# Two programs in one launch: grouped attention's scores as three products of upper parts and rests, with the order of norms, finishes and loads changed

## The reference

```python
def first_block(...):          # two layers; layer 0 mLSTM, layer 1 sliding-window attention
    for i in range(DEPTH):
        u  = _modulate(_rms_norm(h,  norm_mix[i]), mod_l[0], mod_l[1])
        uc = _modulate(_rms_norm(hc, norm_mix[i]), mod_c[0], mod_c[1])
        ...                    # y, yc = _mlstm_mixer(...) or _swa_mixer(...)
        h = h + mod_l[2] * y
        h = h + mod_l[5] * _sq_relu_mlp(_modulate(_rms_norm(h, norm_ffn[i]), mod_l[3], mod_l[4]), w1, w2)
        ...                    # the context alike, in layer 0 only
    return _rms_norm(h, final_norm)

def attend(q, k, v):           # 8 query heads in 2 groups, width 64; queries and keys normed, latents' turned by rope
    s = jnp.einsum('btgrd,blgd->bgrtl', q, k, preferred_element_type=jnp.float32) * (ATTN_HEAD_DIM ** -0.5)
    p = jax.nn.softmax(s, axis=-1)
    return jnp.einsum('bgrtl,blgd->btgrd', p.astype(v.dtype), v)

def trunk_layer(...):          # second program, two layers
    h = x * (1.0 + scale) + shift
    y_attn = blocked_attention(ql, k_all, v_all) * jax.nn.silu(a_g)   # "grouped attention"
    ...                        # y_gla: gated linear attention; y_sgu: spatial gating unit
    out = merge(y_attn, y_gla, y_sgu, m_a, m_g, m_s)
    return layer_norm(DEEPNORM_ALPHA * x + gate * out, p['post_g'], p['post_b'])
```

## Time and profile before

| | |
|---|---|
| median of three runs | 3317.05 us (3314.15 to 3317.81) |
| profiled execution | 3313.33 us; its span 3311.5 us |
| TensorE busy | 3080.0 us, 93% |
| weight loads busy | 2560.9 us, 77% |
| VectorE busy | 1906.8 us, 58% |
| ScalarE busy | 1193.3 us, 36% |
| GpSimd busy | 210.8 us, 6% |
| HBM | 97 GB/s over the span |

### The profile page before, as it was taken

The page is one execution under the profiler, slowest core; times in us unless marked ns, Lnnn a source line. Parts: engine busy times, 40 slices in busy tenths (PEclk is TensorE's granted clock), DMA queues, the critical chain, the costliest instruction groups (busy, mean ns, idle before and its releaser), DMA issues.

```text
span 3311.5 us, 43104 instructions
## 1 busy us (share of the span) xinstructions
PE 3080.0 (93%) x17878; PEld 2560.9 (77%) x17878; DVE 1906.8 (58%) x2778; ACT 1193.3 (36%) x1810; POOL 210.8 (6%) x138
## 2 busy tenths in 40 slices
PE   7998899999997888999989999998899999998899
PEld 6787778888886666778877888886688777876677
DVE  7775646656524475688754444367444565455656
ACT  4225342212223354422235344335322454443432
POOL 0002100000010000000000222000000022200000
PEclk9999899999998899999989999999999999999999
DMA  5454124333321100355523222310212333230223
GB/s 215 154 188 145 39 66 132 126 123 125 111 64 58 39 1 24 130 189 187 184 87 74 78 77 77 114 43 1 86 58 76 109 102 104 98 117 20 70 93 127
DMA packets 100090, 323.91 MB, mean 98 GB/s; under 512 B 14310, under 2 KB 20326, under 8 KB 98744
## 3 DMA queue, kind: packets, MB, share of 16 engines
q1 hardware_dynamic: 89812, 291.29, 27.1%
q10 hardware_dynamic: 10084, 29.87, 2.5%
HBM read 301.46 MB, written 19.66 MB: 97 GB/s over the span
## 4 chain that ended last, share of the span: by engine, by line
PE 80%; DVE 9%; ACT 5%; issue 3%; DMA 1%; POOL 1%; SPq 0%; ACTq 0%; DVEq 0%; POOLq 0%
PE PS L393 79%; PE PS L396 1%; DVE STs L1390 1%; ACT Pq L1348 1%; ACT whi L198 1%; DVE wlo L212 1%; ACT Ps L1348 1%; DVE STq L1390 1%; DMA Ht<-in_hT 1%; POOL rows L2675 0%; POOL rows L2677 0%; DVE JUNK L546 0%; DVE mH L1160 0%; DVE STs L1397 0%; DVE q0t L2302 0%
## 5 line engine op out<-in xcount | busy, mean ns | idle before, releaser
L393 PE MATMUL PS<-U,whi 128*128 128x512 f32 (+1 forms) x5120 | 1091.3, 361 | 46.4 <-DVE U L673 20.4
L393 PEld LDWEIGHTS PS<-U,whi 128*128 128x128 f32 x5120 | 858.4, 191 | 218.9 <-issue 44.6
L212 DVE TENSOR_TENSOR wlo<-stage,whi 128x1024 fp32r<-128x1024 f32 x339 | 432.3, 1277 | 871.8 <-ACT whi L198 870.9
L198 ACT ACTIVATE whi<-stage 128x1024 fp32r<-128x1024 f32 x339 | 357.3, 1056 | 1031.9 <-PE PS L393 960.1
L393 PE MATMUL PS<-U,wlo 128*128 128x512 f32 (+1 forms) x2560 | 571.4, 356 | 0.0
L393 PEld LDWEIGHTS PS<-U,wlo 128*128 128x128 f32 x2560 | 431.7, 189 | 76.4
L393 PE MATMUL PS<-Y,whi 128*128 128x512 f32 (+1 forms) x2112 | 471.6, 359 | 12.1 <-DVE Y L2324 4.5
L393 PEld LDWEIGHTS PS<-Y,whi 128*128 128x128 f32 x2112 | 358.0, 189 | 79.8 <-issue 5.5
L393 PE MATMUL PS<-whi,U 128*128 128x512 f32 (+2 forms) x1152 | 324.2, 369 | 7.5 <-ACT g1qk L1846 4.6
L393 PE MATMUL PS<-Y,wlo 128*128 128x512 f32 (+1 forms) x1056 | 265.6, 358 | 0.0
L393 PEld LDWEIGHTS PS<-whi,U 128*128 128x128 f32 x1152 | 206.5, 190 | 49.2 <-ACT g1qk L1846 5.0
(11 more groups left out here) (433 smaller groups left out, 3137.9 us busy)
## 6 DMA issues: line engine op xcount, KB each, us to landing
stage<-in_w SPq DMA_DIRECT2D x128, 512.0 KB, 4.0
stage<-in_ada SPq DMA_DIRECT2D x80, 512.0 KB, 3.8
stage<-in_adb SPq DMA_DIRECT2D x48, 512.0 KB, 3.8
stage<-in_p_mg SPq DMA_DIRECT2D x16, 512.0 KB, 3.7
stage<-in_p_ma SPq DMA_DIRECT2D x16, 512.0 KB, 3.7
stage<-in_p_ms SPq DMA_DIRECT2D x16, 512.0 KB, 3.7
stage<-in_wo SPq DMA_DIRECT2D x16, 512.0 KB, 3.6
GS<-FS ACTq DMA_DIRECT2D x20, 384.0 KB
```

The lines of the kernel that those rows point to most:

```text
L198: act.activation(self.parts[r % n][0], self.stage[i % len(self.stage)], ACT.Copy).then_inc(*self.S.up("w_hi", i))
L212: dve.tensor_tensor(lo, self.stage[i % len(self.stage)], hi.bitcast(F32), ALU.subtract).then_inc(*self.S.up("w_lo", i))
L393: return pe.matmul(o, l, r, start=start, stop=stop_, skip_group_check=True)
```

## The change

Grouped attention's scores become three products of fp32r parts (`passes`): upper query·upper key, upper·rest, rest·upper. The queries' and keys' parts are made in the projections' stage; the queries' lie in `Y4`, where the results come later. SWA keeps float32, with one pass. The order in the attention loop changes: ScalarE's `finish` goes ahead of its copy of the turned weights; VectorE's is parted into `take` (the gating, grouped attention only) and `finish`, one round later. SWA's masks become one product of the identity with a band of up to 384 columns a head. In norms 0, 1 and 2 the first block is made in two parts, latents first. The final norm and the entry are interleaved, and the modulation there moves from VectorE to ScalarE. In mLSTM two of VectorE's rests of weights come between the scans. SP loads two tiles fewer before SWA's tables. `B.n` is set differently in SWA and grouped attention. In the grouped projections the turn comes one step later and a third gate tile goes into the loop.

```diff
-        def pe_pair(pe, tiles, x, xt):
+        def pe_pair(pe, tiles, x, xt, first=None):
 
 
             ss = [B.take(pe, i, *until) for i, _, until in tiles]
-            for k in range(8):
+            if first:
+                for a, b in cols(True):
+                    pe.wait_ge(*at(*(xt[0] if a else first)))
+                    for (i, _, _), s in zip(tiles, ss):
+                        wh, wl = W.views(i, 8)
+                        if a == 0:
+                            pe.wait_ge(*at("w_lo", i))
+                        for q, (xr, wv) in enumerate(((0, wh), (1, wh), (0, wl))):
+                            mm(pe, s[:, a:b], wv[:, 0, :], x(xr, 0, a, b), q == 0, False)
+            for k in range(1 if first else 0, 8):
...
-            for k in range(9):
+            if full:
+                for lo, hi, v in groups(True):
+                    part = (r, 0) if v else (r, "a")
+                    act.wait_ge(*at("n_mul", *part))
+                    act.activation(T1[0][:, lo:hi], T1[0][:, lo:hi], ACT.Identity, bias=mod(L, ish, 0, v),
+                                   scale=MU[:, 8 * v:8 * v + 1]).then_inc(*up("n_mod", *part))
+                    act.wait_ge(*at("n_mod", *part))
+                    act.activation(U[:, 0, 0, lo:hi], T1[0][:, lo:hi], ACT.Copy).then_inc(*up("n_hi", *part))
+            for k in range(1 if full else 0, 9):
...
+                if k == 0 and full:
+                    for lo, hi, v in groups(True):
+                        dve.tensor_tensor(T1[0][:, lo:hi], HT[:, 0, lo:hi], B.of(("root", r))[:, lo:hi], ALU.mult).then_inc(
+                            *up("n_mul", r, 0 if v else "a"))
+                elif k < 8:
                     if k >= 4:
                         dve.wait_ge(*at("n_lo", r, k - 4))
                     dve.tensor_tensor(T1[k % 4][:, 0:N], HT[:, k, 0:N], B.of(("root", r))[:, 0:N], ALU.mult).then_inc(
                         *up("n_mul", r, k))
-                if k >= 2:
+                if k == 1 and full:
+                    first(0, LAT, (r, "a"))
+                if k == 2 and full:
+                    first(LAT, TOK, (r, 0))
+                elif k >= 2:
...
+            dve_lo(dve, T("mqk", 0))
             gate(dve.tensor_tensor(mAR[r40, :], mIR[r40, :], mF[r40, :], ALU.subtract))
             gate(dve.memset(mMR[r40, :], 0.0))
             both(mMR, mAR, ALU.max)
+            dve_lo(dve, T("mqk", 1))
             gate(dve.tensor_tensor(mMM[r40, :], mF[r40, :], mMR[r40, :], ALU.add))
 
             for rows, c0, c1, before in ((slice(0, 8), 1, 4, 127), (slice(0, 8), 0, 1, 767), (slice(0, 8), 5, 6, 639),
@@ -1080,7 +1114,7 @@
                 top = chunks_of(mMR[rows, :])[:, :, end:end + 1].to_broadcast([8, 6, 128])
                 ins = dve.tensor_tensor(chunks_of(mWR[rows, :]), chunks_of(mAR[rows, :]), top, ALU.subtract)
             ins.then_inc(*up("m_rows"))
-            for j in range(8):
+            for j in range(2, 8):
...
-                            for h, s in enumerate(ss):
-                                last = mm(pe, s[:, c:c + m], a.query(gi, j, h, q0), a.keys(gi, h, k0, m), c % 512 == 0, True)
+                            for i, (query, keys_) in enumerate(a.passes):
+                                for h, s in enumerate(ss):
+                                    last = mm(pe, s[:, c:c + m], query(gi, j, h, q0), keys_(gi, h, k0, m),
+                                              c % 512 == 0 and i == 0, True)
                             c, k0, kn = c + m, k0 + m, kn - m
-                    for c, mask in masks:
+                    for n_, l, r in masks:
                         for s in ss:
-                            last = mm(pe, s[:, c:c + 128], mask[0], mask[1], False, True)
+                            last = mm(pe, s[:, 0:n_], l, r, False, True)
...
-                if n == 3:
-                    rest(act)
+                if n in (3, 4):
+                    rest(act, n - 3)
...
+                if 0 <= n - 2 < N and (n - 2) % 4 == 3:
+                    finish(act, (n - 2) // 4)
...
-        def dve_attention(dve, a, behind, rest, finish):
+
+        def dve_attention(dve, a, behind, rest, take, finish):
+
+
 
             N = len(a.jobs)
-            for n in range(N + 2):
-                if n == 3:
-                    rest(dve)
+            for n in range(N + 3):
+                if n in (3, 4):
+                    rest(dve, n - 3)
...
+                if 0 <= n - 3 < N and (n - 3) % 4 == 3:
+                    finish(dve, (n - 3) // 4)
...
+                if 0 <= n - 2 < N and (n - 2) % 4 == 3 and take:
+                    take(dve, (n - 2) // 4)
...
-                    if j >= 6:
-                        B.n = j
+                    if j == 6:
+                        B.n = 0
                     pe_proj(pe, T("sqk", j), xU, False, ("s_qk", j))
                 if n:
                     r = S_ORDER[n - 1]
-                    if j == 7:
-                        B.n = 0
                     pe_rope(pe, ("s", r), sRM[:, :], swa_turned(r), ("s_qk", r))
...
+            act.wait_ge(*at("ctx_in"))
+            act.wait_ge(*at("u_gain", 0, 1))
             for k in range(9):
                 if k < 8:
                     a = UN[k % 4]
-                    dve.wait_ge(*at("h_final", k))
+                    act.wait_ge(*at("h_final", k))
+                    if k >= 4:
+                        act.wait_ge(*at("u_lo", 0, k - 4))
                     for lo, hi, v in groups(True):
-                        ins = dve.tensor_scalar(a[:, lo:hi], HT[:, k, lo:hi], MU[:, 8 * v + k:8 * v + k + 1],
-                                                mod(2, 0, k, v), ALU.mult, ALU.add)
+                        ins = act.activation(a[:, lo:hi], HT[:, k, lo:hi], ACT.Identity, bias=mod(2, 0, k, v),
+                                             scale=MU[:, 8 * v + k:8 * v + k + 1])
                     ins.then_inc(*up("u_mod", 0, k))
                 if k:
-                    dve.wait_ge(*at("u_hi", 0, k - 1))
-                    dve.tensor_tensor(U[:, 1, k - 1, :], UN[(k - 1) % 4], U[:, 0, k - 1, :].bitcast(F32),
-                                      ALU.subtract).then_inc(*up("u_lo", 0, k - 1))
+                    act.wait_ge(*at("u_mod", 0, k - 1))
+                    act.activation(U[:, 0, k - 1, :], UN[(k - 1) % 4], ACT.Copy).then_inc(*up("u_hi", 0, k - 1))
...
+            dve_root(dve, 4, 4)
+            dve.wait_ge(*at("root", 4))
+            for k in range(10):
+                if k < 8:
+                    dve.scalar_tensor_tensor(HT[:, k, 0:LAT], HT[:, k, 0:LAT], col("final_norm", k),
+                                             B.of(("root", 4))[:, 0:LAT], ALU.mult, ALU.mult).then_inc(*up("h_final", k))
...
+                self.KS = [place(n + "kh", [128, TOK], F32R, offY2)[:, :], place(n + "kl", [128, TOK], F32R, offZ + 34848)[:, :]]
+
+                def query(r):
+                    return lambda gi, j, h, q0: Y4[64 * h:64 * h + 64, r, j, q0:q0 + 128]
+
+                def keys(r):
+                    return lambda gi, h, k0, m: self.KS[r][64 * h:64 * h + 64, k0:k0 + m]
+
+                self.attn = Attention(n, o1, 1, tiles, [(query(0), keys(0)), (query(0), keys(1)), (query(1), keys(0))],
                                       lambda gi, h, b: self.V[:, b, 64 * h:64 * h + 64])
...
-            for n in range(7):
+            for n in range(8):
+                if n == 7:
+                    B.n = 0
                 if n < 5:
                     pe_proj(pe, T(f"p_aqk{L}", n), xU, G.wide_at(n), ("q_z", L, n))
                 else:
@@ -2219,18 +2282,17 @@
                     for a, b in cols(m == TOK):
                         last = mm(pe, s[:, a:b], BONES, x[:, a:b], True, True)
                     last.then_inc(*up("q_ms", L, n - 1))
-                if n >= 2:
-                    if n == 2:
+                if n >= 3:
+                    if n == 3:
                         pe.wait_ge(*at("rot_in", L + 1))
-                    pe_rope(pe, (L, n - 2), G.RM, G.z(n - 2)[0][:, 0:512], ("q_nz", L, n - 2))
-            B.n = 2
-            for j in range(2, 4):
-                pe_proj(pe, T(f"p_ag{L}", j), xU, G.full, ("q_g", L, j))
+                    pe_rope(pe, (L, n - 3), G.RM, G.z(n - 3)[0][:, 0:512], ("q_nz", L, n - 3))
+            B.n = 3
+            pe_proj(pe, T(f"p_ag{L}", 3), xU, G.full, ("q_g", L, 3))
 
             def behind(pe):
                 pe_values(pe, ("q_v", L), [T(f"p_av{L}", 0)], 128, ("q_v", L))
 
-            pe_attention(pe, G.attn, {0: [("r_done", L, 4)]}, behind, ("q_v", L), lambda m: ("q_y", L, m))
+            pe_attention(pe, G.attn, {0: [("q_lo", L, 4)]}, behind, ("q_v", L), lambda m: ("q_y", L, m))
...
+            def upper(j):
+                act.wait_ge(*at("r_done", L, j))
+                act.activation(G.split(j, 0), G.z(j)[0], ACT.Copy).then_inc(*up("q_hi", L, j))
...
+                if n >= 5:
+                    upper(n - 5)
...
```

(20 more changed lines are left out.)

119 lines of the change are left out of this document (57 added, 62 removed).

## The result

| | before | after |
|---|---|---|
| median (executions) | 3317.04 us (4) | 3258.82 us (4: 3258.67 to 3261.75) |
| profiled execution | 3313.33 | 3258.96, span 3257.2 |
| TensorE busy | 3080.0, 93% | 3071.3, 94% |
| mean granted clock | 0.970 | 0.973 |

The ratio is 0.9828, with a 95% interval of 0.9811 to 0.9845: faster by 58, where 71 had been forecast. The time lies inside the forecast's range, 12.8 above its value. Nearly all of the promised gains are there, and one loss that the forecast doesn't have. The profiled execution lies 16.8 above the 3242.1 that the forecast's sum gives for it; 15.4 of that is this one loss.

What follows compares the result with a forecast made beforehand. TensorE's own work and standstills were taken as the bound, with four fifths of the chain. Terms summed to 71.2 off the profiled 3313.33, giving 3242.1; with 3.7 for the median, 3246 us, forecast range 3232 to 3260.

Steps and rivals of the forecast that it cites:

- 6.8 for 6.6: mLSTM: moving two rests of weights between the scans removes a 5.01 wait and its half clock; 6.6 us gained.
- 3.2 for 3.3: Final norm and entry: interleaving lets TensorE start earlier; 3.3 us gained, bounds 0 and 5.
- the two SWA terms: SWA's start: earlier table transfers gain 10.3 us, a new order of PSUM slots gains 11.1.
- 1.9 three times: Norms 0, 1 and 2: first block in two parts gains 1.9 us for each norm, 5.7 together.
- The score's price: Grouped attention: a wide score as twelve matmuls takes 1.35 us instead of 1.56 in plain fp32.
- The term of 2.9: Grouped attention: faster scores shorten the loop period by 0.12 us for each of 24 wide jobs, 2.9 gained.
- the prediction's lower bound, 1.1: Grouped attention: a wide score takes 1.1 us if the heads run side by side, as in the kernel before.
- the second bill: Any TensorE gap: the matmuls after it run at half clock, costing about 1.6 us beside the idle time.
- The two bounds of that part, −2 and 8: Grouped projections: limits around a gain of 5.3 us, 4 in layer 1 and 1.3 in layer 0.
- (a): Rival, grouped scores: heads no longer side by side, a score takes 2.2 us, total 3262; chance 0.11.
- (b): Rival, whole kernel: half of the removed waits given back at the next supplier, total 3281; chance 0.17.
- (c): Rival, attention loops: clock stays low with less TensorE work, slower by 57 us, total 3374; chance 0.03.

Runs made afterwards that it cites:

- e10_norm_fill: e3_keys_first plus idle fp32 products on TensorE in the gaps of the norms and the entry; median 3237.21 us, ratio 0.9753.
- e4_fp32: Changed kernel with grouped scores in plain fp32 as before and without the ten splits; median 3248.06 us, ratio 0.979.
- e3_keys_first: Changed kernel with VectorE doing the key's turn and rest earlier at the end of the grouped projections; median 3245.69 us, ratio 0.9783.
- e1_fill: Changed kernel with eight 512-column products on TensorE ahead of layer 1's first grouped score; median 3242.47 us, ratio 0.9777.
- e12_long_wait_fill: e11_long_wait with sixteen 512-column products between layer 1's first grouped score and the value products; median 3255.42 us, ratio 0.9813.
- e6_loads_back: Changed kernel with SP's two more weight loads ahead of SWA's tables, as before; median 3262.94 us, ratio 0.9843.
- e9_heads_apart: Changed kernel with one head's three products ahead of the other's in each piece of a grouped score; median 3262.46 us, ratio 0.9834.
- e5_fill_behind: Changed kernel with sixteen 512-column products between layer 1's first grouped score and the value products; median 3246.84 us, ratio 0.9795.
- e7_slots_back: Changed kernel with the order of PSUM slots in SWA as before; median 3254.69 us, ratio 0.9831.
- e8_finish_back: Changed kernel with the finishes of both attention loops where they stood before; median 3275.08 us, ratio 0.9885.
- e11_long_wait: Changed kernel with layer 1's first grouped score also waiting for the last gate product; median 3261.46 us, ratio 0.983.
- e2_gap: Kernel before the change, with layer 1's first grouped score also waiting for the last gate product; median 3323.83 us, ratio 1.0029.

## Why the prediction was right, and where it failed

**The stalls named were real, and their sizes nearly so.** Waits that a row shows with its releaser, and whose cause the edit removes, came back as gains: 6.8 for 6.6, 10.5 for 10.3, 10.5 for 11.1, 3.2 for 3.3, and undoing the two SWA terms one by one cost 10.3 and 9.0. In the norms the net gain is 4.8 to 5.8 for 5.7, but not 1.9 three times: norm 0 gave 2.4, the other two 1.1 and 1.3. With the gap filled (e10_norm_fill) the next block binds, as worked out.

**The score's price was right, its reason wasn't, and its meaning is small.** It took 1.31 for 1.35, and the period fell to 4.72, a little below the 4.75 that was taken for VectorE's bound. The term of 2.9 was low by about 3, as 4.97 − 4.72 = 0.25 over 24 jobs is 6. e4_fp32, without the products and without the splits in the projections, comes within 2.4 of e3_keys_first; that the splits take most of these 6 back follows from it, but wasn't measured by itself. The 1.35 was taken for twelve weight loads one after another, 0.110 each. The rows of the score show another pattern: the pairs of 512 columns start 0.23 apart, those of 256 columns 0.12 (2241.57 to 2241.69), where two loads one after another would make it 0.22 for both. So the heads run side by side at the pace of their columns, which is the sum of the prediction's lower bound, 1.1; the other 0.2 is the start of the first pair and the end of the last, which no term had. The near hit is luck. The Trainium skill, "TensorE: Matmul & The Clock Gate", section "LDWEIGHTS (loading the stationary operand)", gives 128/1.2 = 107 ns for a load, and so an estimate of 1.28 for twelve of them one after another. The 1.31 lies near it, but the 0.12 of a pair shows that they aren't one after another here.

**The step that failed** is in the first part: "so the second bill is about 1.6 us". It was taken from sixteen products of 512 columns and used for every gap. In the grouped projections VectorE's last subtractions were named as what would end last and priced at 1.3; the wait is 1.79, but its second bill was 15.4, because 144 products of 128 columns follow. The two bounds of that part, −2 and 8, don't hold it either. e1_fill and e3_keys_first take the wait away and reach 3242.5 and 3245.7, around the 3246 that was forecast. e12_long_wait_fill keeps an even longer wait and has the value products at 1.00 all the same: the low clock over them carries the cost, and not the wait. That the total still lies in the forecast's narrow range, 3232 to 3260, by 1.2 us, with a loss of 15.4 that it doesn't have, is luck too.

**Rivals.** (a) is refuted by the profile after. (b), half of the waits given back, is wrong as a rule, though the one large loss looks like it from the total alone. (c) named the right mechanism, a clock that stays low, and the wrong place: the grouped loops' granted clock, 0.93 and 0.92 before, is 0.98 and 0.96 in the windows after (layer 0, layer 1; the third number from the end), and the stage that fell is the one without any gap in it.

```profile
2972.75:3045.00 72.25, 60.66 (x650) 52.74 (x648) 60.70 (x119) 43.23 (x74) 0.00 (x0) 0.96 0.01 1
2193.50:2289.40 95.90, 74.61 (x818) 62.36 (x817) 76.68 (x177) 56.17 (x114) 0.00 (x0) 0.98 0.01 1
```

The rival was argued against with the narrow jobs, 11.66 of 18.00 busy at 1.00, which show that sparse work holds a high clock; they say nothing on whether it raises a low one.

**Left open.** Why the same wait drops the clock in one execution and not in another isn't settled. Among the profiled executions it did in the changed kernel, e6_loads_back and e9_heads_apart, and it didn't in e5_fill_behind, e7_slots_back and e8_finish_back, with the wait at 1.79 or 1.80 and products of the same kind ahead of it in all six. By the times it did in four of four executions of the changed kernel, two of four of e6_loads_back, one of four of e7_slots_back and perhaps two of four of e8_finish_back. So the choice isn't in the length of the wait.

## What to carry to other kernels

Price a gap on TensorE by what follows it. Here sixteen products of 512 columns took 1.6 us longer when the clock fell among them and had it back at their end, and 144 products of 128 columns stayed low for their whole length, at a cost of 15. Before a stage like the second, let no wait stand, or put wide products (idle ones, if need be) into the wait or between it and the stage. And part a change that comes as a bundle: the three products, which give this one its name, cost it 11 by their wait and are worth 2 without it, within the spread; everything else, without them, brings 69 (e4_fp32).

## What the runs showed of the hardware

- TensorE without a gap can stay at half clock: in the changed kernel the window over the value products alone, 2939.62 to 2970.50, has 30.88 us busy of 30.88 at 0.50 (144 products of 128 columns, 30.88/146 = 0.21 apart). The same products hold 1.00 for 16.2 when they meet it (0.11 apart). The Trainium skill, "TensorE: Matmul & The Clock Gate", section "What's actually happening", has it that activity of the engine releases the throttle; here an engine that the records show as busy throughout didn't, and the measurement decides.
- Which of the two happens behind the same 1.79 wait changes from one execution to another: three of six profiled executions have the fall (Left open), and e6_loads_back has two times at 3255 and two at 3271 with nothing between.
- The clock can fall after the wait, while TensorE is at work again: 0.3 us behind the start of the score in the changed kernel, 1.6 in e11_long_wait and 1.7 in e12_long_wait_fill (by granted clock in windows of half a us). In e2_gap it was low from the score's start.
- Products for the two halves of the rows start in pairs in the records, 3 to 42 ns apart, and the block lasts as long (1.31 and 1.32), also where the program has three for one half ahead of three for the other (e9_heads_apart). Whether the chip or a step of compilation pairs them isn't shown. The Trainium skill, "TensorE: Matmul & The Clock Gate", section "The mechanism", says that products start and end in program order; this trace looks otherwise, with that reservation.
- Idle products of plain fp32 in the norms' gaps paid for themselves, 8.5 in five places by the medians (e10_norm_fill against e3_keys_first), although none of their results is used.
